# Hybrid trunk layer on one core: the SSD running sums as two products of rounded high and low parts of the steps, in place of one native fp32 product

## The chip, the cores and the metric

The kernel runs on one core of a Trainium2 chip. A core has TensorE (matrix products, 128 x 128 array), VectorE, ScalarE, GpSimd and SyncE, each with its own instruction queue; they are ordered only by semaphores. Data lies in SBUF (128 partitions), matrix products are written to PSUM (8 banks of 128 x 512 fp32 numbers). The metric is the device time of one execution in microseconds, the median of several runs; lower is better.

## The reference

One layer of a hybrid encoder on 1024 tokens of width 1024. An input projection feeds three mixers (windowed pooling, a Mamba-2 SSD mixer with 6 heads, and stick-breaking attention with 6 heads); an output projection and a layer norm follow, then a gated feed-forward part with a short convolution and a second layer norm. The change concerns the SSD mixer alone. Per head h, with the step `adt = dt * a` of every token, the scan needs the running sum within a chunk, and the differences of two running sums:

```
a_cum = jnp.cumsum(jnp.moveaxis(adt, 2, -1), axis=-1)
...
seg = a_cum[..., :, None] - a_cum[..., None, :]
decay = jnp.where(causal, jnp.exp(jnp.where(causal, seg, 0.0)), 0.0)
...
y_diag = jnp.einsum('bcgrls,bcsgrp->bclgrp', cb[:, :, :, None] * decay, xdt)
...
y_off = jnp.einsum('bclgn,bcgrpn,bcgrl->bclgrp', cc, h_prev, jnp.exp(a_cum))
```

The kernel computes with chunks of 128 tokens, eight of them (`MT`).

## The kernel before, in words

All tokens stay on the core. Big products are done in the rounded type `float32r`: each operand is split into a rounded high part (`_hi`, made by ScalarE) and the rest (`_lo`, made by VectorE, which subtracts), and three products hi x hi, hi x lo, lo x hi are added up in PSUM (`three`, L734). Small products take the fp32 operands as they are ("native"); in the trace one native product leaves two weight loads and two MATMUL records, a rounded one leaves one of each. Transposes leave one each.

The order of the work is fixed at build time. Stage one is a loop over 90 ticks (and two more) in which attention and input projection are interleaved. It ends with a barrier: TensorE, ScalarE and VectorE call `arrive` (L482), and they and GpSimd wait with `others` (L486). Then comes the SSD stage. Its TensorE work is a list of tasks (`TASKS`, L273 to L276), run in the order in which they stand there, and each writes one of four pairs of PSUM banks (the numbers in `PAIR_OF`); a task waits until the pair's former content has been read (`bank_pair`, L880; `evacuated`, L891):

```
PAIR_OF = {"xt1": 1, "bt0": 2, "xt0": 0, "bt1": 3, "xt2": 0, "cu0": 1, "xt3": 0, "st0": 3, "cu1": 2, "cb0": 0,
           "st1": 1, "st2": 3, "cu2": 0, "st3": 2, "cu4": 1, "cb1": 2, "cu3": 3, "cu5": 2, "yy0": 0, "po0": 3,
           "yy1": 1, "yy2": 2, "po1": 0, "rm0": 3, "sp0": 2, "sp2": 3}
```

- `xt` (L966) turns x back to tokens by rows, six transposes each. VectorE multiplies it by dt (`x_dt`, L1800), and GpSimd multiplies that by the decay to the chunk's end (`x_weighted`, L2305, eight operations). Later on GpSimd's queue stands a multiply of the gating (L2276).
- `bt`, `cb` (L959, L962): B turned back, and the products of C and B; ScalarE copies both out of PSUM (L1380, L1384).
- `cu0` to `cu5` (L953): the running sums of a head, 8 products. The stationary operand is one column of the steps `sm[:, 5, :]`, broadcast to 128 columns; the moving operand is the table `tri_le` (one where row <= column). So every row of the result holds the running sum along the chunk. ScalarE reads it twice: `from_start` (L1386) takes its exponential into `c_scaled` (L1394), and, once TensorE has added a mask (`mask`, L895; L900), `between` (L1396) takes that of the differences into `decayed` (L1405, eight operations a head). ScalarE's order is the calls at L1415 to L1435. `c_scaled` of head 5 waits for VectorE's third `decayed` call (`wt_done`, L1393).
- `st` (L971): states of the chunks; VectorE adds them up in order (`states`, L1833, L1834). In between VectorE splits attention outputs (`mix_lo`, L1821).
- VectorE's `decayed(h)` (L1804) multiplies both results of a head by C·B and by C (L1808, L1809). `yy` (L977) multiplies by them. What follows is gating, pooling (`po`, L987, read by `mix_lo` L1848), the RMS norm, and then the output projection (`out_rows`, L904), whose first rows wait for the last task of their pair of banks.

The steps are made in stage one on VectorE (L1780, semaphore `dt_v`). The table `cap_gt` (L325) is read for the last time by the attention's masking (L1746), in stage one on VectorE. Buffers get their addresses one after another from `put` (L303).

Of the kernel before, what the change touches and what calls it, by code (L numbers as in the profile page):

```python
# [19 lines left out]
F32 = mybir.dt.float32  # L20
F32R = mybir.dt.float32r
I32 = mybir.dt.int32
SIGN = -2 ** 31
ALU = mybir.AluOpType
ACT = mybir.ActivationFunctionType

P = 128
# [8 lines left out]
SSD_HEADS = 6  # L36
# [251 lines left out]
DTN = MT * SSD_HEADS  # L288
# [9 lines left out]
def build(nc, ctx, a, out):  # L298

    kb = 1024  # L300
    top = [2 * kb]

    def put(name, shape, dt=F32, at=None):  # L303

        size = -(-4 * int(np.prod(shape[1:])) // 32) * 32
        if at is None:
            at = top[0]
            top[0] += size
        assert at + size <= 229368, (name, at, size)
        return nc.alloc_sbuf_tensor_at(name, shape, dt, offset=at)  # L310

    def sem(name):
        return ctx.enter_context(nc.semaphore(name))
# [9 lines left out]
    zero = put("zero", [P, 1])  # L323
    rms_eps = put("rms_eps", [P, 1])
    cap_gt = put("cap_gt", [P, P])  # L325
    ident_r = put("ident_r", [P, P], F32R)
    pool_w = put("pool_w", [P, 2, P])
    par = put("params", [P, N_PARAMS])
    sm = put("small", [P, 10, DTN])
# [91 lines left out]
    def table(name):  # L421
        return tab[:, TABLES.index(name), :]
# [23 lines left out]
    dt_v = sem("dt_v")  # L446
# [2 lines left out]
    d_full = sem("d_full")  # L449
    d_free = [sem("d_free%d" % i) for i in range(4)]  # L450
    decay_done = sem("decay_done")
    cexp_done, masked, wt_done = sem("cexp_done"), sem("masked"), sem("wt_done")
    xdt_done = sem("xdt_done")
    xw_done = sem("xw_done")
# [31 lines left out]
    def others(eng):  # L486

        eng.wait_ge(barrier, 3)
# [242 lines left out]
    def _(eng):  # L731
        mm = nc.tensor.matmul
# [155 lines left out]
        def turn(dst, src):  # L888
            return nc.tensor.transpose(dst, src, table("ident"))

        def evacuated(name):  # L891
            pair, before = task_place(name)
            eng.wait_ge(d_free[pair], before + 1)

        def mask(h):  # L895

            eng.wait_ge(cexp_done, h + 1)
            dst = two(task_place("cu%d" % h)[0])
            for b in range(2):
                last = mm(dst[:, b * HALF:(b + 1) * HALF].rearrange("p (k n) -> p k n", k=4), ident_r[:, :],  # L900
                          mask_r[:, :].unsqueeze(1).broadcast_to([P, 4, P]), start=False, stop=True, skip_group_check=True)
            last.then_inc(masked, 1)

        def out_rows(m, kts):  # L904

            if kts[0] == OUT_ORDER[0] and m < 2:
                pairs = [task_place(name) for name in TASKS]
                eng.wait_ge(d_free[m], max(b + 1 for q, b in pairs if q == m))
                eng.wait_ge(sb_split, 3)
            t = slice(m * P, (m + 1) * P)  # L910
            for kt in kts:
                eng.wait_ge(split_done, UNIT[("out", kt)] + 1)
                if kt < 2:
                    evacuated("po%d" % kt)
                elif kt < 5:
                    eng.wait_ge(ssd_split, (3, 2, 4).index(kt) + 1)
                for h in range(2):
                    c = slice(h * HALF, (h + 1) * HALF)
                    last = three(two(m % 2)[:, c], mh[:, kt, t], ml[:, kt, t], oh[kt][:, c], ol[kt][:, c],
                                 kt == OUT_ORDER[0], kt == OUT_ORDER[-1])  # L920
            return last

        for name in TASKS:
            kind, i = name[:2], int(name[2])
            if name == TASKS[1]:
                others(eng)
            if name in MASK_BEFORE:
                mask(MASK_BEFORE[name])
            if kind == "cu":
                eng.wait_ge(dt_v, 2)  # L930
            elif kind == "bt":
                eng.wait_ge(silu_done, 3 + i + 1)
            elif kind == "cb":
                eng.wait_ge(silu_done, 5 + i + 1)
            elif kind == "xt":
                eng.wait_ge(silu_done, 3)
            elif kind == "st":
                eng.wait_ge(xw_done, 2 * (i + 1))
                evacuated("bt0")
                evacuated("bt1")  # L940
            elif kind == "yy":
                eng.wait_ge(wt_done, 2 * (i + 1))
                evacuated("st3")
            elif kind == "po":
                eng.wait_ge(pooled, 2)
            elif kind == "rm":
                eng.wait_ge(sq_done, 2)
            elif kind == "sp":
                if i == 0:
                    out_rows(0, (5, 6, 7))  # L950
                    out_rows(1, (5, 6, 7))
            dst = bank_pair(name)
            if kind == "cu":  # L953

                for c in range(MT):
                    col = sm[:, 5, c * SSD_HEADS + i:c * SSD_HEADS + i + 1]
                    last = mm(dst[:, c * P:(c + 1) * P], col.broadcast_to([P, P]), table("tri_le"),
                              start=c % 4 == 0, stop=False, skip_group_check=True)
            elif kind == "bt":  # L959
                for c in range(MT):  # L960
                    last = turn(dst[:, c * P:(c + 1) * P], cv[:, 3 + i, c * P:(c + 1) * P])
            elif kind == "cb":  # L962
                for c in range(MT):
                    t = slice(c * P, (c + 1) * P)
                    last = mm(dst[:, t], cv[:, 3 + i, t], cv[:, 5 + i, t], start=True, stop=True)
            elif kind == "xt":  # L966
                for c in range(2):
                    for j in range(3):
                        last = turn(dst[:, c * HALF + j * P:c * HALF + (j + 1) * P],
                                    cv[:, j, (2 * i + c) * P:(2 * i + c + 1) * P])  # L970
            elif kind == "st":  # L971
                for c in range(2 if i < 3 else 1):
                    for g in range(2):
                        w = SSD_W // 2
                        last = mm(dst[:, c * HALF + g * w:c * HALF + (g + 1) * w], bn[:, g, 2 * i + c, :],
                                  xw[:, 2 * i + c, g * w:(g + 1) * w], start=True, stop=True)
            elif kind == "yy":  # L977
                for c in range(MT):
                    if i == 0 and c in MASK_INSIDE:
                        mask(MASK_INSIDE[c])  # L980
                    t = slice(c * P, (c + 1) * P)
                    for hd in range(2):
                        r = slice(HEAD * hd, HEAD * hd + HEAD)
                        f = slice((2 * i + hd) * HEAD, (2 * i + hd + 1) * HEAD)
                        mm(dst[r, t], xdt[:, c, f], wt[2 * i + hd][:, t], start=True, stop=False)
                        last = mm(dst[r, t], hs[:, c, f], ce[2 * i + hd][:, t], start=False, stop=True)
            elif kind == "po":  # L987
                for h in range(2):
                    s_ = slice(h * HALF, (h + 1) * HALF)
                    last = mm(dst[:, s_], pool_w[:, i, :], ht[:, 10 + i, s_], start=True, stop=True)  # L990
            elif kind == "rm":

                for j in range(3):
                    if j == 2:
                        eng.wait_ge(sq_done, 3)
                    for h in range(2):
                        s_ = slice(h * HALF, (h + 1) * HALF)
                        last = mm(dst[:, s_], table("rms_%d" % j), cv[:, 3 + j, s_], start=j == 0, stop=j == 2)
            elif kind == "sp":
                for h in range(2):  # L1000
                    s_ = slice(h * HALF, (h + 1) * HALF)
                    if i == 0:
                        eng.wait_ge(rms_done, h + 1)
                    last = mm(dst[:, s_], table("from_last" if i else "from_first"), tmp[:, s_],
                              start=True, stop=True)
            last.then_inc(d_full, 1)
        for kt in OUT_ORDER[3:]:
            for m in range(2):
                last = out_rows(m, (kt,))
# [650 lines left out]
    def _(eng):  # L1660
        v = nc.vector
        chained = [0]

        def link(ins):

            chained[0] += 1
            ins.then_inc(dve_chain, 1)
            eng.wait_ge(dve_chain, chained[0])
# [122 lines left out]
        def evacuated(name):  # L1791
            pair, before = task_place(name)
            eng.wait_ge(d_free[pair], before + 1)

        eng.wait_ge(dt_a, 4)
        for k in X_ORDER:
            src, free = task("xt%d" % k)
# [364 lines left out]
        c = LASTC  # L2162
# [243 lines left out]
```

## Time and profile before

| | |
|---|---|
| median of 3 runs | 1275.12 us (1274.4 to 1275.44) |
| the profiled execution | 1276.14 us |
| its span in the profile | 1274.4 us |
| TensorE busy | 1253.2 us, 98% |
| VectorE, ScalarE, GpSimd busy | 67%, 40%, 9% |
| granted TensorE clock over the span | 0.999 |

The profile is one execution. The span runs from the first to the last instruction; the execution's own time has 1.7 us more around it. Matrix products overlap in the pipeline, so the difference of two starts tells more than the duration of a record, and busy time is the union of the records. "Idle before" is the time an engine stood still ahead of an instruction, with the one that released it.

### The profile page before, as it was taken

How to read it: one execution, taken by the hardware profiler on the slowest of the kernel's cores; microseconds unless marked ns; L12 is line 12 of the kernel's file. 1: busy time of each engine (PE TensorE's matmuls, PEld its weight loads, DVE VectorE, ACT ScalarE, POOL GpSimd, SP SyncE). 2: the span in 40 equal slices, each digit the busy share in tenths (PEclk: the TensorE clock that was granted, in tenths of full speed). 3: DMA queues.
4: the chain of work that ended last, by engine and by line, in shares of the span. 5: the costliest groups of instructions: out<-in, count | busy, mean ns of one | idle time of the engine just before them, and what ended most of it. 6: DMA issues, size and time to landing. Idle time of an engine off the chain costs nothing.

```text
span 1274.4 us, 16374 instructions
## 1 busy us (share of the span) xinstructions
PE 1253.2 (98%) x6120; PEld 1011.3 (79%) x6120; DVE 858.9 (67%) x1090; ACT 515.6 (40%) x794; POOL 114.0 (9%) x69
## 2 busy tenths in 40 slices
PE   7999999999999999999999999999999999999997
PEld 6777777777886888888778888888888888888886
DVE  4546656646397546634787878777787778787863
ACT  5435535547674225213433332424232423233441
POOL 0000000062300002600000000000000000000018
PEclk9999999999999999999999999999999999999999
DMA  6111101110004122110220211112111211010113
GB/s 245 50 34 34 33 33 34 33 50 17 1 1 151 64 70 83 63 34 7 77 67 33 67 37 63 49 49 66 34 65 52 77 35 66 33 66 33 66 58 125
DMA packets 22804, 71.94 MB, mean 56 GB/s; under 512 B 2528, under 2 KB 2784, under 8 KB 22752
## 3 DMA queue, kind: packets, MB, share of 16 engines
q1 hardware_dynamic: 22752, 71.22, 16.3%
q8 instruction: 36, 0.59, 0.2%
q14 instruction: 16, 0.13, 0.0%
HBM read 67.02 MB, written 4.19 MB: 56 GB/s over the span
## 4 chain that ended last, share of the span: by engine, by line
PE 46%; DVE 4%; issue 1%; ACT 1%; DMA 0%; DVEq 0%; SPq 0%; ACTq 0%
PE ps L1090 9%; PE ps L1091 9%; PE ps L1092 9%; PE ps L736 5%; PE ps L737 5%; PE ps L738 5%; PE ps L1130 1%; PE ps L1128 1%; PE ps L1129 1%; DVE w_lo L607 1%; DVE conv_ff L1994 1%; PE ps L1116 1%; DVE conv_ff L1990 1%; ACT conv_ff L1515 0%; DVE conv_ff L2001 0%
## 5 line engine op out<-in xcount | busy, mean ns | idle before, releaser
L736 PE MATMUL ps<-x_hi,w_hi 128*128 128x512 f32 x336 | 139.1, 414 | 7.9 <-DVE x_lo L1711 7.2
L1090 PE MATMUL ps<-mix_hi,w_hi 128*128 128x512 f32 x352 | 137.3, 390 | 1.9 <-DVE partial L2021 1.8
L1091 PE MATMUL ps<-mix_lo,w_hi 128*128 128x512 f32 x352 | 137.0, 389 | 0.0
L1092 PE MATMUL ps<-mix_hi,w_lo 128*128 128x512 f32 x352 | 137.0, 389 | 0.0
L738 PE MATMUL ps<-x_hi,w_lo 128*128 128x512 f32 x336 | 132.4, 394 | 0.0
L737 PE MATMUL ps<-x_lo,w_hi 128*128 128x512 f32 x336 | 131.8, 392 | 0.0
L736 PE MATMUL ps<-h_hi,w_hi 128*128 128x512 f32 x288 | 112.5, 391 | 0.7 <-DVE acc L2042 0.6
L737 PE MATMUL ps<-h_lo,w_hi 128*128 128x512 f32 x288 | 112.1, 389 | 0.0
L738 PE MATMUL ps<-h_hi,w_lo 128*128 128x512 f32 x288 | 112.1, 389 | 0.0
L2042 DVE TENSOR_TENSOR acc<-acc,ps 128x512 f32<-128x512 f32 x144 | 94.6, 682 | 24.9 <-PE ps L738 24.5
L602 ACT ACTIVATE w_hi<-weight_sums 128x512 fp32r<-128x512 f32 x44 | 27.8, 632 | 200.5 <-PE ps L738 149.9
L1090 PE MATMUL ps<-t_hi,w_hi 128*128 128x512 f32 x264 | 103.1, 391 | 0.9 <-DVE w_lo L607 0.7
L1092 PE MATMUL ps<-t_hi,w_lo 128*128 128x512 f32 x264 | 102.7, 389 | 0.0
L1091 PE MATMUL ps<-t_lo,w_hi 128*128 128x512 f32 x264 | 102.7, 389 | 0.0
L1735 DVE TENSOR_TENSOR_SCAN ps<-ps,zero 128x1024 f32<-128x1024 f32 (+7 forms) x48 | 65.4, 1362 | 43.2 <-ACT ps L1294 43.0
L1515 ACT ACTIVATE conv_ff<-ps,params 128x1024 f32<-128x1024 f32 x44 | 53.1, 1208 | 87.9 <-DVE ps L2028 50.4
L736 PEld LDWEIGHTS ps<-x_hi,w_hi 128*128 128x128 f32 x336 | 63.7, 189 | 23.4 <-DVE x_lo L1711 7.2
L2327 POOL TENSOR_TENSOR o_norm<-o_norm,ln_gain 128x1024 f32<-128x1024 f32 x7 | 16.8, 2394 | 702.1 <-ACT o_norm L1655 702.1
L1090 PEld LDWEIGHTS ps<-mix_hi,w_hi 128*128 128x128 f32 x352 | 66.1, 188 | 16.9 <-DVE partial L2021 2.7
L1990 DVE SCALAR_TENSOR_TENSOR conv_ff<-ps,params,conv_ff 128x1023 f32<-128x1023 f32 x44 | 56.4, 1281 | 32.4 <-ACT conv_ff L1515 32.3
L1092 PEld LDWEIGHTS ps<-mix_hi,w_lo 128*128 128x128 f32 x352 | 66.1, 188 | 13.9
L1091 PEld LDWEIGHTS ps<-mix_lo,w_hi 128*128 128x128 f32 x352 | 66.1, 188 | 13.5
(264 smaller groups left out, 2652.5 us busy)
## 6 DMA issues: line engine op xcount, KB each, us to landing
raw<-u_up SPq DMA_DIRECT2D x44, 512.0 KB, 3.3
raw<-u_in SPq DMA_DIRECT2D x22, 512.0 KB, 3.2
down_raw<-u_down SPq DMA_DIRECT2D x38, 256.0 KB, 2.8
x_stage<-u_x SPq DMA_DIRECT2D x8, 512.0 KB, 8.8
raw<-u_out SPq DMA_DIRECT2D x8, 512.0 KB, 3.2
x_nat<-x_nat SPq DMA_DIRECT2D x8, 512.0 KB, 3.3
raw<-u_gate SPq DMA_DIRECT2D x8, 512.0 KB, 3.2
out<-o_norm SPq DMA_DIRECT2D x7, 512.0 KB, 2.6
```

Of the source, the lines that this page charges most:

```text
L602: nc.scalar.activation(op_place(c, o, pp, False), op_raw(c, o, pp), ACT.Copy).then_inc(op_hi_done, 1)
L736: mm(dst, w_hi, x_hi, start=first, stop=False)
L737: mm(dst, w_hi, x_lo, start=False, stop=False)
L738: return mm(dst, w_lo, x_hi, start=False, stop=last)
L1090: mm(dst, w_h[:, k], t_h[:, kt, :], start=fresh and kt == 0, stop=False, skip_group_check=True)
L1091: mm(dst, w_h[:, k], t_l[:, kt, :], start=False, stop=False, skip_group_check=True)
L1092: last = mm(dst, w_l[:, k], t_h[:, kt, :], start=False, stop=kt == 3, skip_group_check=True)
L1515: act(cf[:, r, :], up_row(pp, r), ACT.Identity, scale=column(w, 12, it), bias=column(b, 4, it)).then_inc(row_tap, 1)
L1735: link(v.tensor_tensor_scan(z[:, ::-1], z[:, ::-1], zero[:, 0:1].broadcast_to([P, keys]), 1.0, ALU.mult, ALU.add))
L1990: v.scalar_tensor_tensor(out=cf[:, r, 1:], in0=src[:, :S - 1], scalar=column(w + 1, 12, it), in1=cf[:, r, 1:], op0=ALU.mult, op1=ALU.add). ...
L2042: v.tensor_tensor(dst, dst, ps[:, DOWN_BANKS[k % 4], :], ALU.add).then_inc(dn_added, 1)
L2327: link(g.tensor_tensor(on[:, m % 4, :], on[:, m % 4, :], lng[:, :], ALU.mult))
```

## The change

The steps are split on VectorE, after the barrier, into a rounded high part and the rest (`step_r`, two copies of 48 columns), and the triangle is copied into the rounded type (`tri_r`, at the address of `cap_gt`). Each of the 48 native products becomes two rounded ones, high and low part, added up in the same place of PSUM. The `cu` tasks wait for the split (`step_split`) and no longer for the steps. The new buffer `step_r` takes 384 bytes in each partition and moves every buffer behind it.

```diff
+    tri_r = put("tri_r", [P, P], F32R, top[0] - 4 * P)
+    step_r = put("step_r", [P, 2, DTN], F32R)
     ident_r = put("ident_r", [P, P], F32R)
...
             if kind == "cu":
-                eng.wait_ge(dt_v, 2)
+                eng.wait_ge(step_split, 1)
...
             if kind == "cu":
 
                 for c in range(MT):
-                    col = sm[:, 5, c * SSD_HEADS + i:c * SSD_HEADS + i + 1]
-                    last = mm(dst[:, c * P:(c + 1) * P], col.broadcast_to([P, P]), table("tri_le"),
-                              start=c % 4 == 0, stop=False, skip_group_check=True)
+                    for part in range(2):
+                        col = step_r[:, part, c * SSD_HEADS + i:c * SSD_HEADS + i + 1]
+                        last = mm(dst[:, c * P:(c + 1) * P], col.broadcast_to([P, P]), tri_r[:, :],
+                                  start=c % 4 == 0 and part == 0, stop=False, skip_group_check=True)
...
+        v.tensor_copy(tri_r[:, :], table("tri_le"))
+        link(v.tensor_copy(step_r[:, 0, :], sm[:, 5, :]))
+        v.tensor_tensor(step_r[:, 1, :], sm[:, 5, :], step_r[:, 0, :].bitcast(F32), ALU.subtract).then_inc(step_split, 1)
         eng.wait_ge(dt_a, 4)
         for k in X_ORDER:
```

`link` makes VectorE wait for the end of the instruction before it goes on.

## Rows read from the trace of the kernel before

**Rows 1.** The page, head and part 1.
```profile
span 1274.4 us, 16374 instructions
...
PE 1253.2 (98%) x6120; PEld 1011.3 (79%) x6120; DVE 858.9 (67%) x1090; ACT 515.6 (40%) x794; POOL 114.0 (9%) x69
```

**Rows 2.** Instructions of line 957 (count, ns min/median/max, first and last start).
```profile
L957 PE MATMUL ps<-tables,small x96: 271/275/275, 342.5 to 364.2; 128*128 128x128 f32 x96
```

**Rows 3.** Busy time by stretch: its length, then each engine's, clock and DMA.
```profile
370.20:386.90 16.70, 16.35 (x152) 10.55 (x148) 16.54 (x14) 9.26 (x16) 0.00 (x0) 1.00 0.08 28
```

**Rows 4.** Timeline from 358 us: start, length, engine, line, operands, count, [idle before].
```profile
358.89 2.02 PE L965 MATMUL ps<-conv 128*128 128x128 f32 x16 [0.66 <-DVE states L1834]
...
360.75 3.74 PE L957 MATMUL ps<-tables,small 128*128 128x128 f32 x32
...
362.73 1.94 ACT L1394 ACTIVATE c_scaled<-ps 128x1024 f32<-128x1024 f32 x2 [0.76 <-PE ps L957]
...
364.24 0.72 PE L900 MATMUL ps<-mask,ident_r 128*128 128x512 f32 x2
...
365.04 2.18 ACT L1405 ACTIVATE decayed<-ps,small 128x128 f32<-128x128 f32 x8 [0.37 <-issue]
...
365.59 1.22 DVE L1809 TENSOR_TENSOR c_scaled<-c_scaled,conv 128x1024 f32<-128x1024 f32 x1
...
367.06 1.07 ACT L1394 ACTIVATE c_scaled<-ps 128x1024 f32<-128x1024 f32 x1
367.25 1.23 DVE L1808 TENSOR_TENSOR decayed<-decayed,cb 128x1024 f32<-128x1024 f32 x1 [0.44 <-ACT decayed L1405]
...
370.24 1.23 DVE L1808 TENSOR_TENSOR decayed<-decayed,cb 128x1024 f32<-128x1024 f32 x1 [0.62 <-ACT decayed L1405]
...
386.93 0.50 PE L736 MATMUL ps<-wo_hi,mix_hi 128*128 128x512 f32 x1 [0.38 <-DVE mix_lo L1848]
```

**Rows 5.** Timeline, the first running-sum task.
```profile
342.51 1.95 PE L957 MATMUL ps<-tables,small 128*128 128x128 f32 x16
```

**Rows 6.** Timeline at 321 us: products of 48 columns, then an unhidden load.
```profile
321.13 0.30 PEld L770 LDWEIGHTS ps<-small,tables 128*128 128x128 f32 x2
...
321.35 0.30 PEld L771 LDWEIGHTS ps<-small,tables 128*128 128x128 f32 x2
...
321.65 0.50 PE L736 MATMUL ps<-x_hi,w_hi 128*128 128x512 f32 x1
...
321.99 0.40 PE L737 MATMUL ps<-x_lo,w_hi 128*128 128x512 f32 x1
```

**Rows 7.** Timeline at 284 us, TensorE: rounded products of 64 rows, 128 columns.
```profile
284.46 0.22 PE L790 MATMUL ps<-k_hi,q_hi 64*128 64x128 f32 x2
284.52 0.27 PE L790 MATMUL ps<-k_lo,q_hi 64*128 64x128 f32 x2
284.63 0.28 PE L790 MATMUL ps<-k_hi,q_lo 64*128 64x128 f32 x2
```

**Rows 8.** Timeline at 348 us: GpSimd's multiply and VectorE beside it.
```profile
347.99 2.75 POOL L2276 TENSOR_TENSOR h_tiles<-h_tiles 128x1024 f32<-128x1024 f32 x1
...
349.14 3.82 DVE L1821 TENSOR_TENSOR mix_lo<-sb_out,mix_hi 128x1024 fp32r<-128x1024 f32 x2
```

**Rows 9.** Timeline behind the barrier.
```profile
338.85 0.42 POOL L2296 MEMSET states<- 128x384 f32 x1 [8.90 <-ACTq L484]
...
339.23 1.02 DVE L1800 TENSOR_TENSOR x_dt<-ps,small 128x384 f32<-128x384 f32 x2 [11.63 <-PE ps L889]
...
340.66 1.02 DVE L1800 TENSOR_TENSOR x_dt<-ps,small 128x384 f32<-128x384 f32 x2 [0.41 <-PE ps L889]
...
341.37 6.66 POOL L2305 TENSOR_TENSOR x_weighted<-x_dt,small 128x384 f32<-128x384 f32 x8 [2.10 <-DVE x_dt L1800]
```

**Rows 10.** Instructions of lines 1721 and 1701, VectorE's copies into the rounded type.
```profile
L1721 DVE CAST ident_r<-tables x1: 228/228/228, 23.1 to 23.1; 128x128 fp32r<-128x128 f32 x1
...
L1701 DVE CAST w_hi<-w_lo x1: 192/192/192, 246.7 to 246.7; 128x48 fp32r<-128x48 f32 x1
```

More of the change, by code:

```diff
@@ L451, in build @@
     decay_done = sem("decay_done")
+    step_split = sem("step_split")
     cexp_done, masked, wt_done = sem("cexp_done"), sem("masked"), sem("wt_done")
```

## The prediction

> **What bounds the kernel now.** The page comes first. The span is 1274.4 us with TensorE busy for 98% of it [rows 1], so a shorter list of TensorE work looks like shorter time. That reading has to be tested in the stage that is edited. The line of the running sums comes next: 96 records, started between 342.5 and 364.2 us [rows 2]. There are 48 matrix products (six tasks `cu0` to `cu5`, eight blocks each), so one native fp32 product leaves two records. Then the timeline of the stage from 338 to 387 us, engine by engine, with the question which engine is never ahead of its inputs. In the last third it is VectorE: 16.54 of 16.70 us busy, with TensorE's clock at 1.00, its higher level [rows 3], and TensorE's next large group, the output projection, starts when VectorE's last item there lets go of a bank (`mix_lo` L1848, the last row of [rows 4]). VectorE itself waited shortly before: 0.44 and 0.62 us for ScalarE's `decayed` [rows 4]. So the end of the stage hangs on VectorE, VectorE on ScalarE's exponentials of heads 3 and 4, and these on TensorE only through `cu3`, `cu5` and the mask after them. What TensorE saves elsewhere in the stage is worth what these waits let through.
>
> **The matrix products.** Removed are 48 native products of 128 moving columns. Sixteen records of a task take 1.95 us from the first start to the last end, the last alone 0.275 [rows 2, 5], so the spacing is (1.95 - 0.275) / 15 = 0.112 us, a task is 16 x 0.112 = 1.79 us and the six are 10.7 us. Added are 96 products in the rounded type, also 128 columns wide, two for a block, each with its own weight load of 128 columns: again 16 records a task. The question is the spacing of these. The trace has no full-array rounded product this narrow, so it is bounded.
>
> - From below by 0.06 us: the narrow rounded score products of 64 rows start 0.06 us apart once, right after a wide one [rows 7]. That is their streaming, with the weights already there.
> - From above by 0.224 us, what a whole native product takes now.
> - The value I take is 0.109 us, the middle of 0.105 and 0.112. In the same group the next step is 0.11 us [rows 7], and there is a reason for it. The sums' small products L770 and L771 have only 48 columns to stream, yet their loads follow one another at (321.35 - 321.13) / 2 = 0.11 us [rows 6]: a weight load of 128 columns takes that long, whatever is streamed. A rounded product whose load nothing hides shows the same: 0.50 us at 321.65 against 0.40 for its neighbour, 0.10 more [rows 6]. Under a product of 512 columns such a load is hidden. Under 128 columns it isn't, and a second load for every block is just what the change adds.
>
> At 0.109 a task is 1.74 us, 0.05 less than now, and the six save TensorE 96 x 0.003 = 0.3 us. At 0.06 they would save 96 x 0.052 = 5.0 us.
>
> The Trainium skill (TensorE: Matmul & The Clock Gate, section Back-to-back issue gap) gives about 81 ns a product for a stream of load and product pairs at 128 columns. By that the six tasks would be 7.8 us, 2.9 less than now. No row here shows that spacing.
>
> **How much of it reaches the end.** Walking through the stage:
>
> - `cu0` ends at 344.46 (342.51 + 1.95) [rows 5]. Its saving goes to `xt3`, `st0` and so to VectorE, which then arrives earlier at `mix_lo` L1821. There it stands until GpSimd's multiply L2276 is over (347.99 + 2.75 = 350.74): two of them take 3.82 us [rows 8], where one such 128x1024 operation without GpSimd beside it takes 1.22 (L1809, [rows 4]). GpSimd's chain before it runs without a gap from 341.37 [rows 9], released by the second `xt` task, ahead of `cu0`. So nothing before 350.7 passes: 0.
> - `cu1`, `cu2`, `cu4`: their work is done before VectorE's is, since TensorE waits for its `states` ahead of `cb1` (0.66 us at 358.89, [rows 4]): 0.
> - `cu3` and `cu5` (360.75, 32 records) come after that wait. ScalarE waits 0.76 us for `cu3`, and again for the mask L900 at 364.24, which stands behind `cu5`; its exponentials of head 3 start at 365.04 [rows 4]. Both tasks together give 32 x 0.003 = 0.1 us, and head 3 starts that much earlier.
> - Behind it there is a cap. ScalarE's `c_scaled` of head 5 (367.06) needs VectorE's third `c_scaled`, which starts at 365.59 and takes 1.22, so it is done at 366.81 [rows 4]. A hand-over takes 0.08 (the mask ends at 364.24 + 0.72 = 364.96, ScalarE starts at 365.04), so it could start at 366.89, 0.17 earlier. Head 4's exponentials stand behind it and release VectorE at 370.24. So whatever TensorE saves, no more than 0.17 us passes.
> - From 370.24 to 386.93 VectorE is full, and the rest of the kernel moves with it.
>
> The term is -0.1 us (0 to -0.17).
>
> **VectorE's three added operations.** They are two copies (128x128 and 128x48) and one subtraction (128x48), behind the barrier and ahead of the `x_dt` products. Nearest rows: the copy L1721 0.228, the copy L1701 0.192 [rows 10]; I take 0.2 for the subtraction too. The 128x128 copy overlaps its successor, so about 0.14 + 0.19 + 0.03 for the chained wait, and 0.13 until the next can start: 0.5 us from 338.95. Today VectorE passes the barrier at about 338.85 (GpSimd's memset starts then) and its first product at 339.23, when `xt1` is ready [rows 9]; it would start at 339.45 to 339.55, 0.2 to 0.3 late. Behind it are the two products of `xt1`, who free a bank that only `cu0` wants (342.4), and then `xt0`, for which VectorE waits 0.41 us now (340.66, [rows 9]). The delay ends there: 0. Without that cover it would be +0.3. If GpSimd's memset (0.42 us from 338.85) holds the copies up, they are done 0.3 later and 0.1 to 0.2 goes past the cover, into GpSimd's chain from 341.37, and so to the end. If the operations cost nothing, nothing is gained either, since `xt0` is what is waited for. Term 0, bounds 0 to +0.3.
>
> **Waits and buffers.** The wait of the `cu` tasks goes from the steps to `step_split`, which is there at about 339.5, 2.9 us ahead of `cu0`; behind it in TensorE's queue stands everything else, but it doesn't wait. There is no new DMA and no other queue is touched. The copy of the triangle lies on `cap_gt`, last read at the end of the attention, in VectorE's own order. `step_r` moves all later buffers by 384 bytes; no row prices that and I take 0, with 0.5 us either way in the range.
>
> **Sum.** -0.1 + 0 + 0 = -0.1 us. The profiled execution took 1276.14 us (a span of 1274.4 and 1.7 around it); with the change 1276.0. That run is 1.0 above the median of the three timed runs, 1275.12; on their scale the forecast is 1275.0.
>
> **Rivals.**
>
> - *The narrow product streams at its own rate* (0.06 spacing), and the stage is as worked out above. For it: the one step of 0.06 us. Against: the step behind it and the 48-column loads. Time: capped at -0.17, so 1274.95, the same 1275.0 when rounded. TensorE's busy time would tell, the clock on the wall wouldn't. Chance 0.13.
> - *The same, and TensorE's list sets the end after all* (98% busy): all 5.0 us go through, 1270.1. Against it: the waits of [rows 4] and the full VectorE. Chance 0.03. The Trainium skill (FP8 and Floating Point Precision, section TensorE Precision Notes) counts four passes for true FP32; two rounded products instead would halve TensorE's time for these sums, which leads here. The trace agrees with the count: 0.224 us for 128 columns at 2.4 GHz is 4.2 cycles a column.
> - *VectorE's preparation is late* (memset and copies collide): +0.2 on the chain, 1275.2. Chance 0.08.
> - *The narrow rounded product costs as much as a native one* (slower). It would be 0.224 us for each, 0.112 more than a record now, over 96: +10.7 us. All six tasks stand before the mask of head 3, TensorE has 0.7 us of idle time on the way (the wait before `cb1`), so the stage ends +10.0 later and the kernel takes 1285. It decides from a spacing of about 0.112 + 0.7 / 64 = 0.12 us on (64 records stand before `cb1`). Against it: 64-row products of the same width and type follow at 0.11 [rows 7]. For it: no full-array one is in the trace. Chance 0.05.
>
> That the change doesn't do what it says, and two rounded products take as long as one native, is not a rival but the forecast itself: chance 0.71.
>
> **How the numbers follow.** No change means within 0.2%, 2.5 us, about what a measurement of this kernel can tell. The forecast, the capped rival and the late preparation all lie inside: 0.71 + 0.13 + 0.08 = 0.92, less 0.02 for the buffers' new places, so 0.90. Faster: 0.03 and 0.01 of that, 0.04. Slower: 0.05 and 0.01, 0.06. The range: the forecast with 0.17 + 0.5 below and 0.3 + 0.5 above, and the 0.5 us by which the three runs lie around their median: 1273.9 to 1276.3. The rivals at 1270 and 1285 are left out.
>
> **What would show it.** In the changed kernel, the sixteen records of `cu0` should still take 1.9 us and the six about 11.2 of busy time (1.2 and 7: the rival); VectorE's `xt0` product should still start 1.8 us after the memset; the two waits of `decayed` should shrink by 0.1 at most; and the output projection should follow the memset by 48.0 us, as against 386.93 - 338.85 = 48.08 now. The prediction is wrong if the `cu` records are spaced above 0.12 us, or if the output projection moves by more than 0.5 us with TensorE no longer waiting for `mix_lo`.

## The result, and the profile after

The changed kernel takes 1294.72 us (median of 4 runs, 1293.38 to 1296.12); the kernel before took 1274.8 beside it (1274.4 to 1275.44). The ratio is 1.0151, 95% interval 1.0138 to 1.0164: slower by 20 us, where 1275.0 was forecast and 1273.9 to 1276.3 given as the range. The profiled execution took 1293.38 us (before 1276.14). Of the 15 runs below one, e6, gave two executions, of which one took 1567.69 us at a mean granted clock of 0.753 and is left out of the comparison; it was repeated as e15.

The page after, head and part 1, answers to [rows 1]:

```profile
span 1291.6 us, 16377 instructions
...
PE 1272.4 (99%) x6120; PEld 1013.6 (78%) x6120; DVE 860.4 (67%) x1093; ACT 515.2 (40%) x794; POOL 114.0 (9%) x69
```

The span grew by 17.2 us and TensorE's busy time by 19.2, with the same 6120 products. VectorE has its three new instructions. The first question is where in the span that lies. Here is busy time by stretch, cut at GpSimd's memset behind the barrier and at the first product of the output projection; first after, then the same three stretches before (length, then PE, PEld, DVE, ACT, POOL, clock, DMA share, GB/s):

```profile
0.00:340.27 340.27, 332.26 (x1754) 249.33 (x1755) 185.54 (x202) 179.50 (x284) 41.74 (x30) 1.00 0.15 53
340.27:388.32 48.05, 46.64 (x417) 38.57 (x415) 43.51 (x50) 35.95 (x71) 9.78 (x10) 1.00 0.03 9
388.32:1291.60 903.28, 893.55 (x3952) 725.68 (x3952) 631.40 (x842) 299.72 (x439) 62.47 (x30) 1.00 0.18 59
```

```profile
0.00:338.85 338.85, 329.64 (x1754) 249.33 (x1755) 185.93 (x201) 179.75 (x284) 41.77 (x30) 1.00 0.15 53
338.85:386.93 48.08, 46.70 (x418) 38.60 (x416) 42.86 (x47) 36.05 (x71) 9.79 (x10) 1.00 0.03 10
386.93:1274.40 887.47, 876.83 (x3952) 723.37 (x3952) 630.08 (x842) 299.82 (x439) 62.47 (x30) 1.00 0.18 60
```

The edited stage takes 48.05 us, against 48.08 before and 48.0 forecast. The loss is 1.42 us ahead of it (340.27 - 338.85) and 15.81 behind it (903.28 - 887.47), where not one instruction was edited. The number of products is the same there (3952), the clock is 1.00 on both sides, and TensorE is busy 16.7 us longer. So its products take longer at the same clock.

Which ones, the groups by shape show (`x` count | busy us, mean ns of one). After:

```profile
L1095 PE MATMUL ps<-mix_lo,w_hi 128*128 128x512 f32 x352 | 138.9, 395 | 0.0
...
L740 PE MATMUL ps<-x_lo,w_hi 128*128 128x512 f32 x336 | 132.9, 396 | 0.0
...
L740 PE MATMUL ps<-h_lo,w_hi 128*128 128x512 f32 x288 | 113.6, 395 | 0.0
...
L1095 PE MATMUL ps<-t_lo,w_hi 128*128 128x512 f32 x264 | 104.1, 394 | 0.0
...
L740 PE MATMUL ps<-wo_lo,mix_hi 128*128 128x512 f32 x128 | 49.9, 390 | 0.0
```

And the same groups before:

```profile
L1091 PE MATMUL ps<-mix_lo,w_hi 128*128 128x512 f32 x352 | 137.0, 389 | 0.0
...
L737 PE MATMUL ps<-x_lo,w_hi 128*128 128x512 f32 x336 | 131.8, 392 | 0.0
...
L737 PE MATMUL ps<-h_lo,w_hi 128*128 128x512 f32 x288 | 112.1, 389 | 0.0
...
L1091 PE MATMUL ps<-t_lo,w_hi 128*128 128x512 f32 x264 | 102.7, 389 | 0.0
...
L737 PE MATMUL ps<-wo_lo,mix_hi 128*128 128x512 f32 x128 | 49.9, 389 | 0.0
```

The 512-column products whose stationary operand is in the weight rings (`w_hi`, `w_lo`) are longer, those with `mix`, `h` and `t` by 4 to 6 ns and those with `x` by 2 to 4; the output projection, whose stationary operand is `mix` and whose moving one is `wo`, is not. The 192 feed-forward products whose moving operand is in the rings and whose stationary one is `h` slow too (`w_hi,h_lo`: 390 before, 395 after). The starts of the instructions say it without the modelled ends. TensorE's timeline after:

```profile
911.77 0.40 PE L739 MATMUL ps<-h_hi,w_hi 128*128 128x512 f32 x1
...
914.10 0.39 PE L740 MATMUL ps<-h_lo,w_hi 128*128 128x512 f32 x1
```

and before:

```profile
899.65 0.39 PE L737 MATMUL ps<-h_lo,w_hi 128*128 128x512 f32 x1
...
901.24 0.39 PE L738 MATMUL ps<-h_hi,w_lo 128*128 128x512 f32 x1
```

There are ten steps in the first (eleven products, 2.33 us) and seven in the second (eight products, 1.59 us): 0.233 us a product now, 0.227 before. These are means. Before, nearly every step of `mix`, `h` and `t` is 226 or 227 ns; after, they are spread from 228 to 241. The means over all steps between neighbouring products, worked out from the starts, are 232.4 ns after and 226.8 before for `mix`, `h` and `t`, and 232.4 and 228.7 for `x`. The groups are 3 x 352, 3 x 112, 3 x 288 and 3 x 264 products (3048) and 3 x 336 (1008). That is 3048 x 5.6 ns + 1008 x 3.7 ns = 17.1 + 3.7 = 20.8 us, near the 19.2 of busy time and the 20 of the measured time. Not all of it passes: of the 3.7 us of the `x` products, which lie ahead of the edited stage, 1.42 reach the clock, since TensorE's idle time there shrinks from 9.2 to 8.0 us.

### The profile page after: what moved, and what is told of

Its sections match the earlier page's. It is cut to its first block, busy times and chain, and to the rows that moved or that the text cites. A ratio compares the mean times of both kernels' runs of the same rounds, so it can differ in the third digit from the quotient of the medians.

```text
span 1291.6 us, 16377 instructions
## 1 busy us (share of the span) xinstructions
PE 1272.4 (99%) x6120; PEld 1013.6 (78%) x6120; DVE 860.4 (67%) x1093; ACT 515.2 (40%) x794; POOL 114.0 (9%) x69
## 4 chain that ended last, share of the span: by engine, by line
PE 48%; DVE 3%; issue 1%; ACT 1%; DMA 0%; DVEq 0%; SPq 0%; ACTq 0%
PE ps L1094 10%; PE ps L1096 10%; PE ps L1095 10%; PE ps L739 5%; PE ps L741 5%; PE ps L740 5%; PE ps L1132 1%; PE ps L1134 1%; PE ps L1133 1%; DVE w_lo L610 1%; PE ps L1120 1%; DVE conv_ff L2001 0%; DVE conv_ff L1997 0%; ACT conv_ff L1519 0%; DMA down_raw<-u_down 0%
## 5 line engine op out<-in xcount | busy, mean ns | idle before, releaser
L2334 POOL TENSOR_TENSOR o_norm<-o_norm,ln_gain 128x1024 f32<-128x1024 f32 x7 | 16.7, 2389 | 717.4 <-ACT o_norm L1659 717.4
```

The lines of the kernel that those rows point to most:

```text
L2334: link(g.tensor_tensor(on[:, m % 4, :], on[:, m % 4, :], lng[:, :], ALU.mult))
```

## The experiments

All ratios are to the kernel before on the same chip; the ranges in brackets are 95% intervals. "Distance" is the difference of the addresses, within a partition, of a product's stationary and moving operand. Before, the rings start at byte 10240 (`w_hi`) and 22528 (`w_lo`), `x_hi` and `mix_hi` at 48384 and the slots of `h` and `t` at 113920: all multiples of 256. `put("pad", [P, n])` is an unused buffer of 4n bytes.

### First group: the sums or the places

The theory is that the 384 bytes of `step_r` cost it all. The rival is that the new products or VectorE's preparation change the state in which the rest of the kernel runs.

**e1_change_step_at_end**: the whole change, but no buffer moved.

```diff
-    step_r = put("step_r", [P, 2, DTN], F32R)
+    step_r = put("step_r", [P, 2, DTN], F32R, 228608)
```

> The changed kernel in full, but step_r lies behind all other buffers, so none of them moves from its place in the kernel before. Placement theory (the 384 bytes by which step_r moved the later buffers made the wide rounded products slower): the 512-column products are spaced 0.2267 us again and the time is 1274.8 - 0.1, so 1274.0 to 1275.6. Rival, the sums themselves (two rounded products, the split on VectorE, the new wait): 1293 to 1296, as the changed kernel. My prediction's own term for the sums, -0.1 us, is tested here at once.

Measured: 1275.59 us, ratio 1.0002 (0.9993 to 1.0011). Its page and the `mix_lo` group:

```profile
span 1273.6 us, 16377 instructions
...
PE 1252.7 (98%) x6120; PEld 1011.1 (79%) x6120; DVE 858.9 (67%) x1093; ACT 514.9 (40%) x794; POOL 113.9 (9%) x69
```

```profile
L1095 PE MATMUL ps<-mix_lo,w_hi 128*128 128x512 f32 x352 | 137.0, 389 | 0.0
```

The change with the buffer elsewhere costs nothing, and gains nothing.

**e2_before_moved_384**: the kernel before, with nothing of the change but the shift.

```diff
+    put("pad", [P, 96])
     ident_r = put("ident_r", [P, P], F32R)
```

> The kernel before with an unused buffer of 384 bytes where step_r stands in the changed one; the sums are the native ones. Placement theory: 512-column products with ring weights (w_hi, w_lo) are spaced 0.232 us, 1293 to 1296 in all. Rival, the sums themselves: 1274.4 to 1275.4.

Measured: 1295.89 us, ratio 1.0158 (1.0142 to 1.0173). The unused 384 bytes cost what the change cost, in the same groups:

```profile
L1092 PE MATMUL ps<-mix_lo,w_hi 128*128 128x512 f32 x352 | 138.9, 395 | 0.0
```

**e3_before_all_moved_384**: the same pad ahead of the first buffer, so that the rings move too and every distance stays.

```diff
+    put("pad", [P, 96])
     raw = put("raw", [P, RAWS, D])
```

> The kernel before with an unused buffer of 384 bytes ahead of the first one: every buffer moves by 384 bytes, the rings of the weights too, and all distances between buffers stay. If the distance between weights and moving operand counts: 1274.4 to 1275.4, spacing 0.2267. If the place of the moving operand itself counts: 1293 to 1296, spacing 0.232.

Measured: 1275.95 us, ratio 1.0002 (0.9993 to 1.0012). So in this shift the buffers' own addresses don't matter; their distance from the weights does.

**e4_change_moved_512**: the change, the later buffers moved by 512 bytes instead of 384.

```diff
     step_r = put("step_r", [P, 2, DTN], F32R)
+    put("pad", [P, 32])
```

> The changed kernel with 128 unused bytes behind step_r, so that the later buffers move by 512 and not 384 bytes. If it counts modulo 512 (or 256), the spacing is 0.2267 us and the time 1274.0 to 1275.6. If any move away from the old place costs, or the sums do: 1293 to 1296.

Measured: 1275.81 us, ratio 1.0003 (0.9993 to 1.0012). A move by 512 bytes is free. The cause is settled: e1 and e4 contain the whole change and lose nothing, e2 contains none of it and loses all.

### Second group: how far is too far

The kernel before with a pad of another size ahead of `ident_r`, as in e2. The question is whether the loss comes at every distance that isn't a multiple of some size, or grows towards the middle.

> The kernel before, later buffers moved by 128 bytes. The distance between rings and moving operands was 256 modulo 512 and is 384 now, as against 128 in the changed kernel. If it counts modulo 256: spacing 0.232, 1293 to 1297. If only 128 modulo 512 is bad: 1275 to 1276.5.

> The kernel before, later buffers moved by 64 bytes (distance 320 modulo 512, 64 modulo 256). If any distance that is no multiple of 256 is bad: 1293 to 1297. If the loss grows with the distance from a multiple of 256: about half, 1283 to 1288. If a multiple of 64 is enough: 1275 to 1276.5.

> The kernel before, later buffers moved by 32 bytes (distance 32 modulo 256). If any distance that is no multiple of 256 is bad: 1293 to 1297. If the loss grows with the distance: about a quarter, 1279 to 1282. If a distance of 32 bytes is still within what the engine tolerates: 1275 to 1276.5.

> The kernel before, later buffers moved by 256 bytes: the distance of rings and moving operands is 0 modulo 512, where it was 256. If multiples of 256 are all alike: spacing 0.2267 us, 1275 to 1276.5. If 256 modulo 512 is the only good place for the rings (all good runs had it): 1290 to 1297.

> The kernel before, later buffers moved by 192 bytes: 192 modulo 256 of distance, 64 from the next multiple as the run with 64 bytes (1282.7). If the loss depends on how far the distance is from a multiple of 256 on either side: 1281 to 1285. If on the distance upwards alone: anything from 1290 to 1297.

> The kernel before, later buffers moved by 128 bytes, once more, for the spacings at the full clock, which the first profile of it did not have. Modulo 256: spacing 0.232 us, 1293 to 1297.

| moved by (bytes) | run | us | ratio, 95% |
|---|---|---|---|
| 32 | e8 | 1297.58 | 1.0169 (1.0140 to 1.0199) |
| 64 | e7 | 1282.74 | 1.0054 (1.0031 to 1.0076) |
| 128 | e6, one execution | 1293.83 | none |
| 128 | e15 | 1293.61 | 1.0140 (1.0111 to 1.0170) |
| 192 | e14 | 1297.27 | 1.0169 (1.0140 to 1.0199) |
| 256 | e12 | 1274.92 | 1.0000 (0.9990 to 1.0009) |
| 384 | e2 | 1295.89 | 1.0158 (1.0142 to 1.0173) |

256 is as good as 0. Each of the four other remainders within 256 that was tried costs something, 64 only a third of the rest. 64 and 192 differ by 14.5 us, so the loss isn't the same up and down from a multiple of 256, and it doesn't grow towards the middle: 32 costs more than 64. Against the expectations, e7 lies just under the range for half a loss (1283 to 1288), and e8 and e14 lie 0.6 and 0.3 us above the 1297 at which theirs end.

In e7 not every step of a triple pays. Over the `h` products the one from hi x `w_hi` to lo x `w_hi` takes 231.5 ns (226.7 before), the next 225.9 (226.7), the third 229.3 (227.1); `mix` and `t` show much the same. The modelled lengths of the records hide most of it: `mix_lo` of line 1092 has the 389 ns of before, `x_lo` 395 where it had 392.

```profile
L1092 PE MATMUL ps<-mix_lo,w_hi 128*128 128x512 f32 x352 | 136.8, 389 | 0.0
...
L738 PE MATMUL ps<-x_lo,w_hi 128*128 128x512 f32 x336 | 132.6, 395 | 0.0
```

### Third group: which pair of operands

**e9_slot_region_moved_384**: only the slots of `h`, `t` and `wo` move.

```diff
+    put("pad", [P, 96])
     slot0 = top[0]
```

> The kernel before with 384 unused bytes behind x_lo: the region that holds the moving operands of part of the products (the token sums t1, t2, t4, the gated values h, the output weights wo, p and its weights) moves by 384, while the rings w_hi/w_lo and x, mix stay. Distance theory: x and mix with the rings 0.2267 us as before; t and h with the rings 0.232; wo (moving, moved) with mix (stationary, not moved) 0.232, for the first time in any run; p with proj (both moved) 0.227. About 2050 products at +5.7 ns, so +12 us, 1285 to 1290. Rival, only the place of x and mix or of the small tables counts: 1275 to 1276.5.

Measured: 1287.02 us, ratio 1.0094 (1.0078 to 1.0109).

```profile
L1092 PE MATMUL ps<-mix_lo,w_hi 128*128 128x512 f32 x352 | 137.3, 390 | 0.0
...
L738 PE MATMUL ps<-h_lo,w_hi 128*128 128x512 f32 x288 | 113.7, 395 | 0.0
...
L1092 PE MATMUL ps<-t_lo,w_hi 128*128 128x512 f32 x264 | 104.1, 394 | 0.0
...
L738 PE MATMUL ps<-wo_lo,mix_hi 128*128 128x512 f32 x128 | 50.5, 394 | 0.0
```

`h` and `t` are slow, `mix` is not, and the output projection is slow for the first time (232.4 ns a step, 227.1 before): its moving operand `wo` moved and its stationary one `mix` stayed, where in e2 both moved together and nothing was lost. The feed-forward products that stream the ring past a stationary `h` are the case in which the stationary operand is the one that moved, and they are slow too (`w_hi,h_lo` 395 ns, 390 before). So it makes no difference which of the two moves.

**e5_only_w_hi_at_odd_distance** and **e10_only_w_lo_at_odd_distance** ask which product of a triple pays when only one part of the weights is at a distance that isn't a multiple of 256 (called odd from here on).

```diff
     wh = put("w_hi", [P, RINGS, D], F32R)
+    put("pad", [P, 96])      # e5;  e10: 32, and 96 more ahead of "tables"
     wl = put("w_lo", [P, RINGS, D], F32R)
```

> The kernel before with 384 unused bytes between w_hi and w_lo. w_lo and everything behind it moves by 384, so w_lo keeps its distance to the moving operands and only w_hi is off by 384. A triple is x_hi with w_hi, x_lo with w_hi, x_hi with w_lo, and while one product streams, the weights of the next are loaded. Theory load (the load of the next weights meets the stream): 0.232 us from the start of the first and of the third product of a triple to the next start, 0.2267 from the second. Theory own (a product and its own weights): 0.232 from the first and the second, 0.2267 from the third. Both give two thirds of the loss, 1275.5 + 13.5 = 1289 (1286 to 1291); the spacings by kind decide.

> The kernel before with w_lo moved by 128 and everything behind it by 512 bytes: w_hi keeps its distance to the moving operands modulo 512, w_lo is off by 384 modulo 512. In the run with w_hi off, all three products of a triple were slow, the second too, whose next load is w_lo at the old distance, and the third, whose own weights are. If a product is slow when either its own weights or those loaded beneath it are at an odd distance: the first of a triple (w_hi, then w_hi) 0.2267 us, the second and the third 0.232. If the distance between w_hi and w_lo counts: all three slow. If only w_hi counts: none, 1275 to 1276.5.

Measured: e5 1297.24 us, 1.0167 (1.0137 to 1.0196); e10 1290.37, 1.0120 (1.0102 to 1.0139). In e5:

```profile
L739 PE MATMUL ps<-h_hi,w_lo 128*128 128x512 f32 x288 | 114.4, 397 | 0.0
L738 PE MATMUL ps<-h_lo,w_hi 128*128 128x512 f32 x288 | 113.7, 395 | 0.0
L737 PE MATMUL ps<-h_hi,w_hi 128*128 128x512 f32 x288 | 113.4, 394 | 0.6 <-DVE acc L2043 0.4
```

and in e10:

```profile
L740 PE MATMUL ps<-h_hi,w_lo 128*128 128x512 f32 x288 | 114.3, 397 | 0.0
L739 PE MATMUL ps<-h_lo,w_hi 128*128 128x512 f32 x288 | 114.0, 396 | 0.0
L738 PE MATMUL ps<-h_hi,w_hi 128*128 128x512 f32 x288 | 112.3, 390 | 0.5 <-DVE acc L2044 0.4
```

The steps from one start to the next, means over `h` in ns:

| from, to | before | e5 | e10 |
|---|---|---|---|
| hi x w_hi, lo x w_hi | 226.7 | 232.4 | 226.7 |
| lo x w_hi, hi x w_lo | 226.7 | 232.6 | 232.5 |
| hi x w_lo, hi x w_hi | 227.1 | 235.0 | 234.1 |

e5 is a miss for both theories of its expectation: all three steps are slow, though the product with `w_lo` has an even distance, and the time is above both ranges. A rule that fits both runs here is that the step ahead of an odd product and the step behind it both widen. In e5 every step touches a product with `w_hi`. In e10 two of three steps touch the one with `w_lo`, and just these two are slow. By that rule e10 keeps a third of its steps fast. (In both runs `w_hi` and `w_lo` are also at an odd distance from each other, and no run takes that apart.)

**e13_only_x_lo_moved_384** tests the rule on the moving side: only `x_lo` moves.

```diff
     xh = put("x_hi", [P, KT, S], F32R)
+    put("pad", [P, 96])
     xl = put("x_lo", [P, KT, S], F32R)
...
+    put("pad2", [P, 32])
     slot0 = top[0]
```

> The kernel before with x_lo alone moved by 384 bytes (what lies behind it moves by 512, so its distances stay modulo 512). The input projection has 336 triples x_hi with w_hi, x_lo with w_hi, x_hi with w_lo; only while x_lo streams (second) is there an odd distance. Theory spill (the load of the next weights meets the stream, and the delay reaches into the next product as well): 0.232 us from the second and from the third product of a triple, the first as before. Theory pair (a product is slow if its own weights or the next ones are at an odd distance to its own moving operand): only the second is slow. All other stages as before. Time 1275.3 + 2 (pair) or + 4 (spill), 1276.5 to 1280.

Measured: 1277.6 us, ratio 1.0016 (1.0005 to 1.0028). The `mix`, `h` and `t` groups are as before. Of the `x` steps the one ahead of `x_lo` goes from 229.4 to 232.2 ns, the one behind it from 228.0 to 231.6, and the third from 229.1 to 230.6. That is neither of the two expected patterns, which had the first step as before; the rule of both neighbours gives the first two, and the rise of the third is left over. 672 x 3.2 ns = 2.2 us for the two, against 1.75 measured.

The rule doesn't hold everywhere, though. In e9, 43 steps lead from a `mix` product (even) to the first product of `t` or `h` (odd), and they stay at 226.7 ns; the 43 steps from `t` back to `mix` take 229.4. In e5 the step from `w_lo,h_hi` (even) to `w_hi,h_lo` (odd), with the ring moving, stays at 227.2 ns as before. So whether the step ahead of an odd product widens differs from place to place, and the full rule stays open.

### Fourth group: does TensorE's time count in the edited stage

**e11_step_at_end_high_part_only**: e1 without the low part of the steps, 8 products a task in place of 16. It leaves out 48 of the 96 products, and the running sums are those of the rounded steps.

```diff
-                    for part in range(2):
+                    for part in range(1):
```

> The changed kernel with step_r behind all other buffers (nothing moved), without the products of the low part of the steps, so that the running sums lack the low part: 48 products in place of 96 in the cu tasks, about 5.3 us less for TensorE in the stage. Cap theory of the prediction (VectorE and ScalarE let through no more than 0.17 us): 1275.3 to 1275.6 where the kernel before is 1275.5, the output projection 0.2 us earlier behind GpSimd's memset and no more. Rival, TensorE's list sets the end: 1270.2, ratio 0.996.

Measured: 1276.28 us, ratio 1.0012 (1.0003 to 1.0021), against 1275.59 of e1 on another chip. Taking some 5 us of products off TensorE (48 x 0.11) gains nothing. It is 0.7 us above the upper end of what was expected by the cap (1275.3 to 1275.6) and 6 above the rival's 1270.2. From memset to output projection it takes 386.58 - 338.23 = 48.35 us, where e1 takes 385.76 - 337.70 = 48.06. The timeline of e11:

```profile
338.23 0.42 POOL L2303 MEMSET states<- 128x384 f32 x1 [8.90 <-ACTq L487]
...
358.27 2.89 PE L969 MATMUL ps<-conv 128*128 128x128 f32 x16 [1.62 <-DVE states L1841]
...
360.81 2.85 PE L961 MATMUL ps<-tri_r,step_r 128*128 128x128 f32 x16
...
366.90 1.23 DVE L1815 TENSOR_TENSOR decayed<-decayed,cb 128x1024 f32<-128x1024 f32 x1 [0.71 <-ACT decayed L1409]
...
386.58 0.50 PE L739 MATMUL ps<-wo_hi,mix_hi 128*128 128x512 f32 x1 [0.39 <-DVE mix_lo L1855]
```

TensorE arrives at `cb1` sooner and waits there longer (it is busy for 0.66 of the 2.20 us from 356.00), 1.62 us in place of 0.69 in e1. Behind the wait its clock is lower (stretch, length, then as above):

```profile
356.00:358.20 2.20, 0.66 (x2) 0.21 (x2) 2.06 (x5) 1.45 (x6) 0.00 (x0) 1.00 0.00 0
358.20:361.20 3.00, 2.93 (x18) 2.96 (x19) 3.00 (x3) 0.73 (x4) 0.00 (x0) 0.67 0.00 0
361.20:364.00 2.80, 2.58 (x17) 2.44 (x17) 2.80 (x4) 2.23 (x3) 0.00 (x0) 0.74 0.00 0
364.00:370.00 6.00, 6.00 (x71) 4.40 (x71) 4.67 (x5) 6.00 (x20) 0.00 (x0) 1.00 0.01 3
```

A mean of 0.67 and 0.74 is a mix of the upper level (2.4 GHz) and the lower (1.2). `cb1` takes 2.89 us where e1 has 2.02 [rows 4 show 2.02 too], and the sixteen products of `cu3` and `cu5` that remain take 2.85. So the saving of that stretch is gone: the mask of head 3 starts 25.64 us after the memset, where e1 has 25.42, and VectorE's wait for `decayed` of head 3 is 0.71 us instead of 0.43: 0.28, about the 0.29 by which the stage is longer. The profiled execution therefore doesn't show the prediction's cap at work, since no saving arrives at it. This is one execution, with a mean clock of 0.997 over the span. Of the 11 executions four have 0.997, two 0.998 and five 0.999, while all of e1's have 0.999, so the dip comes in some and not in others. Their times don't separate by it (1275.55 to 1279.52 with the lower clock, 1275.59 to 1277.12 at 0.999): what it costs is below what the runs can tell, and that the saving gains nothing doesn't hang on it, since the five at 0.999 are no faster than e1's either. The Trainium skill (Perfetto Trace Analysis, section Matmul Optimizations) says that power is scaled with utilization and that products should run back to back in batches; the trace agrees: in the profiled execution a saving became idle time, and the idle time was followed by a lower clock.

## Why the prediction was wrong

**The step that failed** is in "Waits and buffers": "`step_r` moves all later buffers by 384 bytes; no row prices that and I take 0, with 0.5 us either way in the range". It was +20 us. e2 shows it alone (+20.4), e1 shows all the rest without it (+0.1). The bound of 0.5 us rested on nothing. An honest one would have come from the count: 4056 products with ring weights and 384 of the output projection, so one ns on each is 4.4 us, and bounds of ±1% of a 227 ns step would have been ±10 us. No row of before could have given the sign or size, since all these buffers lay at multiples of 256 bytes.

The other steps:

- *Matrix products.* Forecast: spacing 0.109 us, sixteen records of `cu0` in 1.9 us, the list 0.3 us shorter.

```profile
343.85 1.98 PE L961 MATMUL ps<-tri_r,step_r 128*128 128x128 f32 x16
...
360.30 2.02 PE L969 MATMUL ps<-conv 128*128 128x128 f32 x16 [0.70 <-DVE states L1841]
362.07 3.77 PE L961 MATMUL ps<-tri_r,step_r 128*128 128x128 f32 x32
```

Against [rows 2, 5] the spacing is (1.98 - 0.275) / 15 = 0.114 us, so the list is 96 x 0.002 = 0.2 us longer, not shorter. The 0.109 was the middle of 0.105 and 0.112, and no row gives the 0.105; the rows it leaned on show 0.11. The rivals at 0.06 and at 0.224 are out. The 81 ns of the Trainium skill (TensorE: Matmul & The Clock Gate, section Back-to-back issue gap) don't show either. Its four passes for true FP32 (FP8 and Floating Point Precision, section TensorE Precision Notes) do, in the 0.224 us of a native product [rows 2, 5], but two rounded products didn't halve the time: they take 2 x 0.114 us.

- *VectorE's preparation.* The rows answer to [rows 9]:

```profile
340.24 0.52 DVE L1799 CAST tri_r<-tables 128x128 fp32r<-128x128 f32 x1 [11.32 <-ACTq L487]
340.27 0.42 POOL L2303 MEMSET states<- 128x384 f32 x1 [9.01 <-ACTq L487]
340.38 0.41 DVE L1800 CAST step_r<-small 128x48 fp32r<-128x48 f32 x1
340.82 0.21 DVE L1801 TENSOR_TENSOR step_r<-small,step_r 128x48 fp32r<-128x48 f32 x1
340.95 2.15 DVE L1807 TENSOR_TENSOR x_dt<-ps,small 128x384 f32<-128x384 f32 x4
...
342.79 6.66 POOL L2312 TENSOR_TENSOR x_weighted<-x_dt,small 128x384 f32<-128x384 f32 x8 [2.10 <-DVE x_dt L1807]
```

The collision did come: beside the memset the copies took 0.52 and 0.41 us, where [rows 10] have 0.228 and 0.192. `x_dt` starts 0.68 us after the memset (0.38 before), 0.3 late. But its four products now run in one go, without the 0.41 us of waiting, and GpSimd's chain starts 2.52 us after the memset, as before (341.37 - 338.85). The three operations took 0.71 us up to `x_dt`, where 0.5 was forecast, but began 0.03 us ahead of the memset and not 0.1 behind it. The cover named was there, and big enough.

- *The path.* ScalarE and VectorE at heads 3 to 5, against [rows 4]:

```profile
364.10 1.94 ACT L1398 ACTIVATE c_scaled<-ps 128x1024 f32<-128x1024 f32 x2 [0.71 <-PE ps L961]
...
368.65 1.23 DVE L1815 TENSOR_TENSOR decayed<-decayed,cb 128x1024 f32<-128x1024 f32 x1 [0.43 <-ACT decayed L1409]
...
371.63 1.23 DVE L1815 TENSOR_TENSOR decayed<-decayed,cb 128x1024 f32<-128x1024 f32 x1 [0.62 <-ACT decayed L1409]
...
388.32 0.50 PE L739 MATMUL ps<-wo_hi,mix_hi 128*128 128x512 f32 x1 [0.38 <-DVE mix_lo L1855]
```

The waits are 0.43 and 0.62, as they were (0.44 and 0.62), and VectorE's `mix_lo` still opens the output projection. The term of -0.1 us measured nothing: the mask of head 3 starts 25.41 us after the memset (365.68 - 340.27), 25.39 before. e11 agrees that TensorE's savings don't pass, but not by how much of the 0.17 us.

What stays open is the mechanism of the loss. The runs show that it comes with the operands' distance, not what in the memory or in TensorE's reads makes it so, nor the full rule for which of two neighbouring steps widens (e9, e13), nor why 64 is milder than 32 and 192. No kernel tried beats the one before: e1, e3, e4 and e12 all lie within 0.1% of it.

## What to carry to other kernels

A new buffer is an edit of every product whose operands it moves apart: put it behind all others, or round its size up (here to 256 bytes), and test a placement alone before blaming the arithmetic. When a term multiplies thousands of instructions, its bound is a nanosecond times their count, not a token half microsecond. And work that is taken off an engine ahead of a wait becomes idle time, which gains nothing and can be followed by a lower clock (e11).

## What the runs showed of the hardware

- A rounded 128x512 product with its own weight load starts every 0.227 us when stationary and moving operand are a multiple of 256 bytes apart in the partition, and on the mean every 0.232 to 0.235 us at most other distances tried (32, 128, 192, 384); with 64 the three steps of a triple take 0.226 to 0.232 (e7). Moving both operands together by 384 bytes costs nothing (e3), and a product at a multiple of 256 is slow too between others that aren't (e5).
- Products of 256 columns from the same buffers didn't slow: the group `mix_lo,w_hi` 128x256 has a mean of 282 ns after and 283 before, and they start 0.119 us apart after and 0.120 before.
- Products of 128 columns with a load each, rounded or native halves, start every 0.112 to 0.114 us.
- After a wait of 1.62 us, and 0.66 us of work in the 2.2 us up to its end, TensorE ran at a mean clock of 0.67 and 0.74 for 5.8 us in the profiled execution of e11, and the mean clocks of five of the ten others are lower too; after 0.70 us idle it kept 1.00.
- VectorE's copy of 128x128 took 0.52 us beside GpSimd's memset and 0.228 without.
